# A mixture-of-experts stage whose matmul units wait for a two-part weight: order of the products, and place of two read-outs

## The reference, cut to what matters

```python
gate, idx = lax.top_k(aff.T, cap)             # 16 experts, 80 token slots each (64 latent, 16 context)
xe = xt[idx]
hid = jax.nn.silu(jnp.einsum('ecd,edf->ecf', xe, w_g)) * jnp.einsum('ecd,edf->ecf', xe, w_u)
ye = jnp.einsum('ecf,efd->ecd', hid, w_d) * gate[..., None].astype(xe.dtype)
out = jnp.zeros_like(xt).at[idx.reshape(-1)].add(ye.reshape(-1, D_MODEL))
```

## Time and profile before

| | us |
|---|---|
| median of 3 runs | 3112.13 (3110.88 to 3113.62) |
| the profiled execution | 3106.49, its span 3104.9 |
| TensorE busy | 2979.4 (96%), 20078 matmuls |
| VectorE busy | 2172.0 (70%) |
| ScalarE busy | 1417.7 (46%) |
| mean granted TensorE clock | 0.986 of full speed |
| chain that ended last | PE 78%, DVE 8%, DMA 7%, ACT 3%, issue 3% |

### The profile page before, as it was taken

How to read it: one execution, slowest core, us unless ns; L and a number is a source line. 1 busy time by engine, 2 the same in 40 slices (tenths; PEclk the granted TensorE clock), 3 DMA queues, 4 the chain that set the end, 5 groups by cost and what they waited for, 6 DMA issues and landing times.

```text
span 3104.9 us, 50675 instructions
## 1 busy us (share of the span) xinstructions
PE 2979.4 (96%) x20078; PEld 2511.3 (81%) x20078; DVE 2172.0 (70%) x2406; ACT 1417.7 (46%) x1627; POOL 299.3 (10%) x449
## 2 busy tenths in 40 slices
PE   6999999999999999999999997899999999999997
PEld 4899999989999999999999996566666666666664
DVE  5777776566666666674244334899998999999997
ACT  3322233333333333333122222577777777777775
POOL 0011110011111111110011111000000000000001
PEclk9999999999999999999999998899999999999998
DMA  9544442454545454553345435899999999999994
GB/s 399 226 144 129 133 124 95 171 207 160 203 167 198 179 184 177 188 182 111 128 166 193 135 105 197 307 381 386 372 383 386 386 391 386 389 379 371 385 396 149
DMA packets 131269, 756.45 MB, mean 244 GB/s; under 512 B 17552, under 2 KB 27840, under 8 KB 56656
## 3 DMA queue, kind: packets, MB, share of 16 engines
q1 hardware_dynamic: 98832, 636.54, 53.6%
q0 software_dynamic: 32272, 117.53, 12.3%
HBM read 686.87 MB, written 60.58 MB: 241 GB/s over the span
## 4 chain that ended last, share of the span: by engine, by line
PE 78%; DVE 8%; DMA 7%; ACT 3%; issue 3%; POOL 0%; DVEq 0%; SPq 0%; ACTq 0%; POOLq 0%
PE pu L1145 29%; PE pu L773 10%; PE pu L774 10%; PE pu L775 10%; PE pt L752 2%; PE pu L855 2%; PE pt L955 2%; PE pu L858 2%; PE pu L857 2%; DMA raw<-in_w_ada 2%; ACT ehi L1543 2%; DMA blocks<-in_w_in 2%; PE ps L855 1%; PE ps L858 1%; PE ps L857 1%
## 5 line engine op out<-in xcount | busy, mean ns | idle before, releaser
L2306 DVE TENSOR_TENSOR elo<-ering,ehi 128x2048 fp32r<-128x2048 f32 x384 | 871.5, 2288 | 104.8 <-ACT ehi L1543 101.4
L1543 ACT CAST ehi<-ering 128x2048 fp32r<-128x2048 f32 x384 | 731.3, 1912 | 249.1 <-PE pu L1145 248.9
L773 PE MATMUL pu<-hhi,whi 128*128 128x320 f32 x2144 | 680.5, 317 | 5.5 <-DVE hlo L2057 3.9
L775 PE MATMUL pu<-hhi,wlo 128*128 128x320 f32 x2144 | 664.2, 310 | 0.0
L774 PE MATMUL pu<-hlo,whi 128*128 128x320 f32 x2144 | 664.1, 310 | 0.0
L773 PEld LDWEIGHTS pu<-hhi,whi 128*128 128x128 f32 x2144 | 404.4, 189 | 14.9 <-issue 9.5
L774 PEld LDWEIGHTS pu<-hlo,whi 128*128 128x128 f32 x2144 | 404.5, 189 | 1.6
L775 PEld LDWEIGHTS pu<-hhi,wlo 128*128 128x128 f32 x2144 | 404.0, 188 | 0.0
L1145 PE MATMUL pu<-ehi,xhi 128*80 128x512 f32 x1024 | 322.8, 396 | 5.1 <-DVE ysl L2333 3.2
L1145 PE MATMUL pu<-ehi,xlo 128*80 128x512 f32 x1024 | 320.6, 394 | 0.0
L1145 PE MATMUL pu<-elo,xhi 128*80 128x512 f32 x1024 | 320.1, 394 | 0.0
(11 more groups left out here) (383 smaller groups left out, 4536.3 us busy)
## 6 DMA issues: line engine op xcount, KB each, us to landing
ering<-in_w_experts SPq DMA_DIRECT2D x384, 1024.0 KB, 8.7
raw<-in_w_ada SPq DMA_DIRECT2D x96, 1024.0 KB, 7.8
blocks<-in_w_in SPq DMA_DIRECT2D x72, 512.0 KB, 4.3
raw<-in_w_in SPq DMA_DIRECT2D x34, 1024.0 KB, 5.0
raw<-in_w_attn_out SPq DMA_DIRECT2D x16, 1024.0 KB, 5.4
raw<-in_w_out SPq DMA_DIRECT2D x16, 1024.0 KB, 4.9
gates_tanh<-th POOLq DMA_DIRECT2D x32, 320.0 KB, 2.4
gl<-gates_tanh POOLq DMA_DIRECT2D x32, 320.0 KB, 3.6
```

What stands on the lines that cost most here:

```text
L773: nc.tensor.matmul(o, whi[:, dk, w:w + 128], hi[:, kt, cols], start=kt == 0, stop=False)
L775: last = nc.tensor.matmul(o, wlo[:, dk, w:w + 128], hi[:, kt, cols], start=False, stop=kt == kts - 1)
L1543: nc.scalar.copy(ehi[:, j % AHEAD, :], ering[:, slot, :]).then_inc(ex_hi, 1)
L2306: nc.vector.tensor_tensor(elo[:, j % AHEAD, :], ering[:, slot, :], ehi[:, j % AHEAD, :].bitcast(F32), ALU.subtract).then_inc(ex_lo, 1)
```

## The change

In TensorE's unit the eight matmuls that read the weight's high part come first, behind a wait for `ex_hi` alone. Then comes the wait for `ex_lo`, and then the four that read the low part. In VectorE's steps 21 and 23 (19 and 23 in the last expert) the read-out is put ahead of the lowering of unit j + 3.

```diff
-                pe.wait_ge(ex_lo, e * EU + (j + 1))
+                pe.wait_ge(ex_hi, e * EU + (j + 1))
                 n = unit_of(j, following)
...
+                k0 = 2 * (n % 8 if h < 2 else n % 4)
+                xh, xl = (xhi, xlo) if h < 2 else (hthi, htlo)
                 for b in range(2):
-                    k = 2 * (n % 8 if h < 2 else n % 4) + b
-                    hi, lo = (xhi[:, k, :], xlo[:, k, :]) if h < 2 else (hthi[:, k, :], htlo[:, k, :])
-                    for left, ring in ((hi, ehi), (hi, elo), (lo, ehi)):
+                    k = k0 + b
+                    for left in (xh, xl):
                         for c in range(2):
                             w = 1024 * b + 512 * c
-                            last = nc.tensor.matmul(pu[0:SLOTS, 2 * (h % 2) + c, :], left, ring[:, j % AHEAD, w:w + 512],
...
+                            nc.tensor.matmul(pu[0:SLOTS, 2 * (h % 2) + c, :], left[:, k, :], ehi[:, j % AHEAD, w:w + 512],
+                                             start=k == 0 and left is xh, stop=False)
+                pe.wait_ge(ex_lo, e * EU + (j + 1))
+                for b in range(2):
+                    k = k0 + b
+                    for c in range(2):
+                        w = 1024 * b + 512 * c
+                        last = nc.tensor.matmul(pu[0:SLOTS, 2 * (h % 2) + c, :], xh[:, k, :], elo[:, j % AHEAD, w:w + 512],
+                                                start=False, stop=k == kts - 1)
                 last.then_inc(ex_mm, 1)
...
+                if j in ((21, 23) if following else (19, 23)):
+                    slots_y(e, int(j == 23), j + 1)
                 if following or j + AHEAD < EU:
                     unit_lo(e, j + AHEAD)
...
-                if j in ((21, 23) if following else (19, 23)):
-                    slots_y(e, int(j == 23), j + 1)
```

More of the change, by code:

```diff
@@ L1138, in expert @@
                 kts = KT if h < 2 else FT
+                k0 = 2 * (n % 8 if h < 2 else n % 4)
+                xh, xl = (xhi, xlo) if h < 2 else (hthi, htlo)
                 for b in range(2):
-                    k = 2 * (n % 8 if h < 2 else n % 4) + b
-                    hi, lo = (xhi[:, k, :], xlo[:, k, :]) if h < 2 else (hthi[:, k, :], htlo[:, k, :])
-                    for left, ring in ((hi, ehi), (hi, elo), (lo, ehi)):
+                    k = k0 + b
+                    for left in (xh, xl):
                         for c in range(2):
                             w = 1024 * b + 512 * c
-                            last = nc.tensor.matmul(pu[0:SLOTS, 2 * (h % 2) + c, :], left, ring[:, j % AHEAD, w:w + 512],
-                                                    start=k == 0 and left is hi and ring is ehi,
-                                                    stop=k == kts - 1 and left is lo)
+                            nc.tensor.matmul(pu[0:SLOTS, 2 * (h % 2) + c, :], left[:, k, :], ehi[:, j % AHEAD, w:w + 512],
[7 more added lines that the diff above has]
+                                                start=False, stop=k == kts - 1)
                 last.then_inc(ex_mm, 1)
```

## The result

The changed kernel takes 3095.01 us (median of 6 runs, 3092.45 to 3096.54), the kernel before 3111.65 (6 runs, 3109.68 to 3113.76). The ratio is 0.9945, 95% interval 0.9932 to 0.9957: 16.6 us faster, with 13.4 to 21.2 as its interval. Forecast were 3100.1 us, a range of 3098 to 3107, and a gain of 12.0. The sign and both places were right. The profiled execution took 3092.8 us, span 3091.2; before it was 3106.49 and 3104.9, so the two profiles differ by 13.7.

A forecast was written before the change was run, and what follows sets the result against it. TensorE was taken to bound the experts. 5.0 + 0.3 (unit 3), 6.2 + 0.25 (boundaries) and 0.3 (tail) gave 12.0 us, and 3112.1 - 12.0 = 3100.1 us, range 3098 to 3107.

The forecast's parts named there:

- What bounds the kernel: In the experts stage TensorE sets the pace: busy 68.60 of 68.95 us an expert, so only its waste can be won.
- the prize: What TensorE wastes in each expert: 68.95 us against 68.15 without waste, so 0.80 us.
- Part 1, place two: TensorE's wait for the low part at unit 3 goes: 0.36 us, 14 times, 5.0 us, plus 0.3 in the first expert.
- The added wait: The extra wait in each unit costs 0 when met; upper end 0.07 us at 384 units, 27 us.
- part 1: New order of the products in TensorE's units, removing unit 3's stall: 5.0 us, plus 0.3 in the first expert.
- count and shape of the matmuls stay: Premise on TensorE's units: still 12 matmuls each, each with its own weight load.
- Part 2, place one: Earlier read-outs remove TensorE's stall between experts: 0.44 us at 14 boundaries, 6.2 us, plus 0.25 at the 15th.
- The open question: At the boundary, whether queue work or the loop's branch makes 0.17 us; branch taken as holding none; rival chance 0.12.
- Part 3, transfers: Weight transfers rise to 389 GB/s from 384, with 15 us in hand; cost 0.
- Part 4, the tail: In the last expert the first read-out passes one lowering, moving the add to HBM and loads some 2.5 us; gain 0.3.
- the wait for the loaded sums: In the tail, VectorE's wait of 0.32 us at 3072.05 for the loads behind the add to HBM.
- the level: Last step for the whole kernel: 5.64 us between profiled execution and median kept, so 3112.1 - 12.0 = 3100.1 us.

The follow-up runs named there:

- e2: Kernel before with only the new product order and the later wait for the low part, read-outs at their old place; 3100.53 us, ratio 0.9977, period 68.52.
- e4: Changed kernel with the wait for the low part back at the unit's start, new product order kept; 3099.91 us, ratio 0.9972, period 68.50.
- e7: Changed kernel with three more waits for the high part in each unit, all met long before; period 68.09 us, executed once at 3096.22 us.
- e3: Kernel before with only the read-outs moved ahead of the lowering, products in the old order; 3102.29 us, ratio 0.9978, period 68.57.
- e8: Changed kernel with the eight high-part products as four with the tokens' high part, then four with their low part; period 68.11 us.
- e1: The changed kernel again, beside the kernel before on one chip; 3093.80 against 3108.46 us, ratio 0.9954, period 68.09.
- e9: Changed kernel with one extra VectorE sum over 1024 columns between the second read-out and the lowering for unit 2; period 68.09 us.
- first pairing: The first two sets of six runs, changed kernel against kernel before; 3095.01 against 3111.65 us, ratio 0.9945.
- e5: Kernel before with 24 dummy matmuls where TensorE waits for the first expert's tokens; 3107.23 against 3107.35 us, ratio 1.000.
- e10: Changed kernel with three extra VectorE sums over 1024 columns between the second read-out and the lowering for unit 2; period 69.44 to 69.50 us.
- e11: The kernel of e4 with one extra VectorE sum over 1024 columns between the second read-out and the lowering for unit 2; period 69.05 against 68.50 us.
- e6: Changed kernel with 24 dummy matmuls where TensorE waits for the first expert's tokens; 3094.81 us, ratio 0.9963.

## Why the prediction was wrong, and where it was right

**What bounds the kernel** was right: in the experts TensorE sets the pace. That the prize is only its idle time was not quite: I put an expert without waste at 68.15 us, and it is 68.09.

**Part 1, place two** was right in place and kind (gone in e2 and after, back in e4, with the table load behind it, as the boundary without one shows). e2's 0.44 less e4's order effect of 0.07 is 0.37, and from e4 to the changed kernel it is 0.41; forecast 0.36. The added wait costs nothing, as forecast (e7).

**What part 1 missed:** from "count and shape of the matmuls stay" I took it that the pace stays, and put the order at nothing without a run behind it. It makes 0.07 us an expert, 1 us in all (e3 against e4). By the mean of the steps in e4's timeline, a matmul in the group of four low parts takes 230.0 ns to the next and one in the pairs 230.7 to 231.0. Why stays open: e8 only rules out that longer groups do it everywhere.

**Part 2, place one** was right. e3 gains 0.39 an expert, I had 0.44 with a restart. The open question, whether the loop's branch holds TensorE, is answered: with the read-out 2.9 us early there is no gap at the branch. The Trainium skill, "Runtime: NRT & Kernel Launch", section "Instruction fetch mechanics", lets a taken branch wait for a DMA fetch where its target is not in the window that is held. In these traces no such fetch shows: there is no gap, and in both kernels only the two data queues have packets.

The parts by themselves give 0.44 + 0.39 = 0.83 and together 0.87. The last 0.04 I can't assign.

**Part 3, transfers,** was right: 389 GB/s after, 384 before, landing times up to 13.3 us against 12.1, and ScalarE waits for no landing.

**Part 4, the tail.** The read-out moved, and the wait for the loaded sums is gone (timeline after):

```profile
3057.27 1.22 DVE L2410 TENSOR_TENSOR fin<-fin,pu 128x1024 f32<-128x1024 f32 x1 [0.49 <-PE pu L1179]
3058.41 1.22 DVE L2414 CUSTOM_DVE_ANT_0 fsv<-fin 128x1024 f32<-128x1024 f32 x1
```

From the one-hot product's start (line 1170, at 3063.70) to the end it was 41.2 us before and 40.4 after, but 40.9 in e1 and 41.2 in e9, so the 0.3 can't be told from scatter.

**The step that failed most is the last one, the level.** I made the sum against the profiled execution, got 3094.5 for its like, and then added 5.64 us, because the median of three runs stood so much higher, saying that no step of mine touches the difference. For the kernel before it did hold in the first pairing: six runs have a median of 3111.65, 5.2 above its profile. But it did not carry over to the changed kernel, whose median beside them was 3095.01, and 3093.80 in e1. Nor did it stay with the kernel before in later pairings: the 23 runs of e1 to e4 have 3108.46 and the 15 of e5 to e8 3107.35, which is 2.0 and 0.9 above the profile. So the term was some 4 to 5 us too large, and that alone takes the forecast below 3098. That 3094.5 lies so near the measured 3095.0 is partly luck, for one execution stood in for the level and the gain was too small.

What lifted the kernel before in the first pairing, and not the changed one, stays open. On which chip that pairing ran is not known. It is hardly the spread alone: the lowest of the six runs is 3109.68, and only 4 of the later 23 and 2 of the 15 reach that.

Within one chip too the executions spread, and the traces show part of where, ahead of the experts, in code that no variant touches. The matmuls of line 1066 (first and last start), in e10 and in e11:

```profile
L1066 PE MATMUL pt<-xres,wrg x160: 272/273/284, 1696.7 to 1914.7; 128*16 128x128 f32 x160
```

```profile
L1066 PE MATMUL pt<-xres,wrg x160: 272/273/285, 1704.2 to 1922.2; 128*16 128x128 f32 x160
```

The last starts at 1914.7 in one and at 1922.2 in the other, 7.5 us apart; in the kernel before it was 1916.5, after 1918.1, in e1 1920.7. The largest single difference in TensorE's waits is that for VectorE's `blo`, 9.5 us in e10 and 13.2 in e11:

```profile
PE pu L855 <- DVE blo L1716: 9.5, 14, 1.8
```

```profile
PE pu L855 <- DVE blo L1715: 13.2, 14, 1.6
```

Why it differs stays open. TensorE's clock differs also. In the same two stretches (length, busy, clock, DMA, GB/s) e10 has

```profile
0.00:100.00 100.00, 63.88 (x1123) 0.98 0.99 406
...
1300.00:1400.00 100.00, 92.74 (x686) 0.98 0.54 198
```

and e11 has

```profile
0.00:100.00 100.00, 64.71 (x1090) 0.95 0.99 403
...
1300.00:1400.00 100.00, 93.77 (x675) 0.95 0.55 202
```

A mean of 0.95 is some 10 us in a hundred at 1.2 GHz, 0.98 some 4, while the program is the same. From 200 to 300 us it is the other way round (0.98 in e10, 1.00 in e11), and how much of the 7.5 us the clock makes is not shown. The clock also enters the comparison of my two profiles: from the tokens' transposes to the first hidden transposes, TensorE's part of the first expert, the kernel before took 33.91 us at a mean clock of 0.87, the changed one 32.37 at 0.91:

```profile
1953.49:1987.40 33.91, 32.75 (x137) 21.11 (x138) 24.91 (x18) 21.78 (x16) 0.93 (x1) 0.87 0.87 311
```

```profile
1954.91:1987.28 32.37, 31.35 (x136) 20.55 (x137) 24.87 (x18) 21.78 (x16) 0.93 (x1) 0.91 0.91 341
```

Of these 1.54 us only unit 3's 0.3, and less than 0.1 by the order, belong to the change. The profiles' 13.7 thus split into -1.5 there, -12.7 from the first hidden transposes to the last, -0.8 in the tail, and +1.4 ahead of the experts. That the clock's moment does not come with the change is read from the rows: e1, the changed kernel again, took 30.2 us from its first unit's start to the first hidden transposes, the first trace of it 28.9 and the kernel before 30.4. No experiment shows it, since e5 and e6 failed to hold the clock.

How large the true gain is: three readings of 16.6, 14.7 and 12.4 us. In the part that repeats to hundredths it is 12.7, and with unit 3 of the first expert 13.0, where the same terms of my sum make 11.75. So the gain was the second step that was mis-sized, about 1.3 us too small, of which the order makes 1. The other 3 to 4 us of the first pairing's 16.6 no trace shows.

The chances were fair on the sign (faster at 0.77). The range was too narrow below: it took in only the uncertainty of the steps and none of the level's.

## What to carry to other kernels

When an operand comes in two parts made one after the other, let each wait stand ahead of the first product that reads its part, and put the late part's products last. A met wait cost nothing here, and the producer gained 1.85 us of room. In a hand-written order of operations, such as VectorE's here, put what another engine waits for next (a read-out that frees a bank) ahead of work wanted later, and check the order against the moment each result is wanted.

For a forecast: price stalls by the step from start to start, and state the level by the spread of runs, not by the distance of one profile from one median.

## What the runs showed of the hardware that was not expected

The order of identical matmuls changed their pace by 0.1%: 22.44 us against 22.41 for 96 matmuls and four transposes (e3 and e4), nearly the same in each expert.

After 24 matmuls over 8 us the clock was at 2.4 GHz, and some 5 us later, after small transposes and the waits between them, unit 0 began at 1.2 GHz (e5).
